# Order of the first loads and products in a fused three-layer transformer kernel

## The reference

```
proj = x @ ab_w_in[0]                    # 256 x 1024 times 1024 x 1440
c_q, c_kv, k_r, q_s, k_s, v_s = split(proj)
q  = rms_norm(c_q, q_norm) @ w_uq        # the low-rank norms
kv = rms_norm(c_kv, kv_norm) @ w_ukv
...
mem_n = rms_norm(mem_2, mem_norm_g_2[0]) # 256 x 1024, used by the third block
mk, mv = split(mem_n @ w_mem_kv_2[0])
```

## Time and profile before

| | |
|---|---|
| median of 3 runs | 922.51 us (921.9 to 922.72) |
| the profiled execution's own time | 924.75 us |
| its span in the trace | 922.6 us |
| granted TensorE clock, mean | 0.997 |
| TensorE busy | 99% of the span |
| VectorE, ScalarE, GpSimd busy | 66%, 55%, 4% |

### The profile page before, as it was taken

One profiled execution on the slowest core, in us unless ns is written; L12 is line 12 of the kernel. 1 busy time (PEld: TensorE's weight loads), 2 busy tenths in 40 slices (PEclk: granted clock), 3 DMA queues, 4 the chain that ended last, 5 costly groups with the idle time before them and its releaser, 6 DMA issues.

```text
span 922.6 us, 12818 instructions
## 1 busy us (share of the span) xinstructions
PE 911.3 (99%) x4766; PEld 765.2 (83%) x4766; DVE 608.7 (66%) x1003; ACT 508.4 (55%) x819; POOL 36.4 (4%) x53
## 2 busy tenths in 40 slices
PE   8999999999999999999999999999999999999997
PEld 6888878888888898877888888887888888888876
DVE  3788687666662766778766666376656577574665
ACT  4876664555552456666455555355457574655444
POOL 1100024100000001000000000001000000000000
PEclk9999999999999999999999999999999999999999
DMA  8664466755574668444755557454564565545651
GB/s 293 238 220 121 122 226 194 262 183 185 192 246 131 146 172 256 137 155 166 256 176 187 195 189 245 125 198 142 185 204 137 160 195 167 163 152 189 197 174 64
DMA packets 72556, 169.39 MB, mean 184 GB/s; under 512 B 11304, under 2 KB 33216, under 8 KB 71856
## 3 DMA queue, kind: packets, MB, share of 16 engines
q1 hardware_dynamic: 69536, 155.83, 52.2%
q0 software_dynamic: 2816, 12.48, 4.1%
q10 hardware_dynamic: 144, 0.26, 0.1%
HBM read 167.49 MB, written 1.06 MB: 183 GB/s over the span
## 4 chain that ended last, share of the span: by engine, by line
PE 95%; DVE 2%; ACT 1%; DMA 1%; issue 0%; SPq 0%; ACTq 0%; DVEq 0%
PE psum L740 21%; PE psum L927 14%; PE psum L693 8%; PE psum L688 8%; PE psum L690 8%; PE psum L931 7%; PE psum L960 7%; PE psum L965 3%; PE psum L851 3%; PE psum L861 3%; PE psum L855 3%; PE psum L1062 2%; PE psum L1093 1%; PE psum L660 1%; PE psum L1076 1%; PE psum L1018 1%
## 5 line engine op out<-in xcount | busy, mean ns | idle before, releaser
L1636 DVE TENSOR_TENSOR base_lo<-stage,base_hi 128x1024 fp32r<-128x1024 f32 (+3 forms) x222 | 262.1, 1204 | 95.1 <-ACT base_hi L1245 94.2
L1245 ACT CAST base_hi<-stage 128x1024 fp32r<-128x1024 f32 (+3 forms) x222 | 223.8, 1035 | 52.4 <-PE psum L693 25.3
L1636 DVE TENSOR_TENSOR extra_lo<-stage,extra_hi 128x1024 fp32r<-128x1024 f32 (+1 forms) x68 | 80.0, 1202 | 47.5 <-ACT extra_hi L1245 47.4
L688 PE MATMUL psum<-base_hi,xt 128*128 128x512 f32 (+2 forms) x272 | 107.8, 396 | 1.6 <-ACT base_hi L1459 0.7
L690 PE MATMUL psum<-base_lo,xt 128*128 128x512 f32 (+2 forms) x272 | 105.2, 387 | 1.2 <-DVE base_lo L1636 0.7
L693 PE MATMUL psum<-base_hi,xt 128*128 128x512 f32 (+2 forms) x272 | 105.3, 387 | 0.0
L1245 ACT CAST extra_hi<-stage 128x1024 fp32r<-128x1024 f32 (+1 forms) x68 | 68.1, 1030 | 49.3 <-PE psum L740 33.5
L740 PE MATMUL psum<-base_hi,ht 128*128 128x512 f32 x288 | 87.3, 393 | 0.0
L927 PE MATMUL psum<-xt,extra_hi 128*128 128x512 f32 x320 | 87.3, 394 | 0.0
L960 PE MATMUL psum<-xt,base_hi 128*128 128x512 f32 x240 | 76.5, 403 | 0.0
L927 PE MATMUL psum<-xt,base_hi 128*128 128x512 f32 x256 | 69.7, 394 | 0.0
(11 more groups left out here) (243 smaller groups left out, 1548.2 us busy)
## 6 DMA issues: line engine op xcount, KB each, us to landing
stage<-in_w_up SPq DMA_DIRECT2D x80, 512.0 KB, 4.5
stage<-in_w_down SPq DMA_DIRECT2D x44, 512.0 KB, 4.5
stage<-in_w_in_a SPq DMA_DIRECT2D x22, 512.0 KB, 4.9
stage<-in_w_cd_in SPq DMA_DIRECT2D x16, 512.0 KB, 4.7
stage<-in_w_in_b SPq DMA_DIRECT2D x12, 512.0 KB, 3.6
stage<-in_w_ab_in SPq DMA_DIRECT2D x11, 480.0 KB, 6.8
ln_par<-in_ln POOLq DMA_DIRECT2D x4, 1024.0 KB, 6.6
stage<-in_w_ab_out SPq DMA_DIRECT2D x8, 512.0 KB, 3.7
```

The costliest lines, as they stand in the source:

```text
L688: pe.matmul(acc, ah, wh, start=(k == 0), stop=False)
L1245: act.copy(w_hi(c, 0, w), stage_of(c, w)).then_inc(hi_done, 1)
L1636: dve.tensor_tensor(w_lo(c, 0, w), stage_of(c, w), w_hi(c, 0, w).bitcast(F32), ALU.subtract).then_inc(lo_done, 1)
```

## The change

SyncE loads x's tile 1 behind chunk 1, ahead of chunks 2 and 3. Column step 0 has three passes: tile 0 by chunks 0 and 1, tile 1 by chunks 0 and 1, both tiles by chunks 2 and 3; the turning of a tile stands ahead of its first pass. ScalarE and VectorE turn and split in the order that goes with it. Memory's norm row, memory and the gains are loaded by SyncE behind chunk 7, and no longer by GpSimd, which still loads the heads' parameters there.

```diff
--- before.py
+++ after.py
@@ -505,6 +505,9 @@
             u = PRODUCTS[name].u0 + steps - 1
             return acc_free[u % 2], TT * (u // 2 + 1)
 
+        def row(src, n):
+            return bass.AP(tensor=src.tensor, offset=src.offset, ap=[[0, P], [1, n]])
+
         block = ctx.enter_context(nc.Block())
 
 
@@ -513,6 +516,13 @@
 
             def load_x(t):
                 sp.dma_start(x[:, t, :], d["x"][t * P:(t + 1) * P, :]).then_inc(loaded[f"x{t}"], 16)
+
+            def load_memory():
+                for name, dst, src in (
+                        ("mem_g", row_g[:, :], row(d["mem_norm_g"], D)),
+                        ("mem", mem_x, d["mem"].rearrange("(t p) n -> p t n", t=TT)),
+                        ("gains", gains, row(d["gains"], Q_RANK + KV_RANK))):
+                    sp.dma_start(dst, src).then_inc(loaded[name], 16)
 
             load_x(0)
             sp.dma_start(ident[:, :], d["ident"]).then_inc(loaded["ident"], 16)
@@ -545,8 +555,10 @@
                         for m, landed in enumerate((first_staged, staged[STAGE[0]])):
                             cut = slice(m * FIRST, (m + 1) * FIRST)
                             sp.dma_start(stage_of(0, WIDTH[0])[:, cut], d["w_ab_in"][0][:, cut]).then_inc(landed, 16)
-                    if g.c0 + n == NS - 1:
+                    if g.c0 + n == 1:
                         load_x(1)
+                    if g.c0 + n == 2 * NS - 1:
+                        load_memory()
             for t in range(TT):
                 for j in range(2):
                     cut = slice(j * 512, (j + 1) * 512)
@@ -562,14 +574,8 @@
             def load(name, dst, src):
                 pool.dma_start(dst, src).then_inc(loaded[name], 16)
 
-            def row(src, n):
-                return bass.AP(tensor=src.tensor, offset=src.offset, ap=[[0, P], [1, n]])
-
             pool.memset(no_mask[:, :], 0.0).then_inc(constants_set, 1)
             pool.wait_ge(hi_done, NS)
-            load("mem_g", row_g[:, :], row(d["mem_norm_g"], D))
-            load("mem", mem_x, d["mem"].rearrange("(t p) n -> p t n", t=TT))
-            load("gains", gains, row(d["gains"], Q_RANK + KV_RANK))
             load("heads", head_par[:, :, :].rearrange("p a h -> p (a h)"), row(d["head_par"], 16))
             pool.wait_ge(hi_done, 2 * NS)
             load("swa", table, d["swa"])
@@ -665,14 +671,15 @@
 
                 u, cps = g.u0 + j, g.kc // g.kp
                 pair = u % 2
-                passes = [(t,) for t in range(TT)] if second else [tuple(range(TT))]
-                for tiles in passes:
-                    if second:
+                passes = [(tuple(range(TT)), range(cps))]
+                if second:
+                    passes = [((0,), range(2)), ((1,), range(2)), (tuple(range(TT)), range(2, cps))]
+                for tiles, chunks in passes:
+                    if second and len(tiles) == 1:
                         second(tiles[0])
                     if u >= 2:
-
-                        pe.wait_ge(acc_free[pair], 2 * (u // 2) - (tiles == (0,)))
-                    for m in range(cps):
+                        pe.wait_ge(acc_free[pair], 2 * (u // 2))
+                    for m in chunks:
                         n = j * cps + m
                         c = g.c0 + n
                         for kk in range(g.kp):
@@ -1454,12 +1461,16 @@
             turn_part(first, "x0")
             act.wait_ge(first_staged, 16)
             act.copy(w_hi(0, 0, FIRST), stage_of(0, FIRST)).then_inc(first_hi, 1)
-            turn_part(last, "x0")
             act.wait_ge(staged[STAGE[0]], 16)
             act.copy(w_hi(0, FIRST, FIRST), stage_of(0, WIDTH[0])[:, FIRST:]).then_inc(hi_done, 1)
             done["chunks"] = 1
+            turn_part(last, "x0")
+            split_to(2)
+            first, last = turn_parts("x0", [1])
+            turn_part(first, "x0")
+            split_to(3)
+            turn_part(last, "x0")
             split_to(NS)
-            turn("x0", xt_hi, 0, [1])
 
             def memory_norm():
                 act.wait_ge(constants_set, 3)
@@ -1972,8 +1983,12 @@
             split_first(1).then_inc(lo_done, 1)
             done["chunks"] = 1
             turn_part(last, xt_hi, xt_lo, 0, "x0")
+            split_to(2)
+            first, last = turn_parts("x0", [1])
+            turn_part(first, xt_hi, xt_lo, 0, "x0")
+            split_to(3)
+            turn_part(last, xt_hi, xt_lo, 0, "x0")
             split_to(NS)
-            turn("x0", xt_hi, xt_lo, 0, [1])
 
             def memory_norm():
                 dve.wait_ge(loaded["mem_g"], 16)
```

## The result

The changed kernel took **925.86 us** (median of 6 runs, 924.27 to 927.07), the kernel before, beside it, 922.06 (6 runs, 921.73 to 922.72). The ratio is 1.0033, 95% interval 1.0021 to 1.0045: slower, by 3.8 us, where 921.9 was forecast with 920.8 to 924.0 as the range. Its traced execution took 927.07 us with a span of 925.1, where the span before was 922.6. Four of all the executions told of here, one of them of the kernel before, took 1130 to 1876 us; they are left out of the ratios and move a median by 0.1 us at most.

The account below looks back on a forecast made before the run. TensorE, busy 99% of the span, was taken as the bound; 0.55 us saved there, all else costing nothing, turned the profiled 924.75 us into 924.2, and the median 922.51 into 921.9, range 920.8 to 924.0.

Parts of the forecast that it names:

- Memory on the weights' queue: Memory's loads on SyncE behind chunk 7: chunk 8 lands at about 28.7 us instead of 27.4, hidden, costing nothing.
- rival B: Memory ahead of chunk 8 delays ScalarE if under 0.37 MB/us: +1.05 us at 300 GB/s, +2.85 at 243; chance 0.15.
- The passes: Column step 0 on TensorE: the new pass order shrinks the hole at tile 1's start from 0.70 to 0.15, saving 0.55 us.
- rival C: Hole before tile 1's first product only moves if TensorE turns tile 1 at full clock; median stays 922.5; chance 0.10.
- Chunks 2 and 3 split later: ScalarE and VectorE split these chunks around tile 1's turn, still 0.7 and 1.5 us early for TensorE; cost nothing.
- Rival A: Transposes in the 1.2 GHz stretch keep TensorE's clock low for longer: +1.0 us, 923.5; chance 0.16.
- Rival D: TensorE's clock doesn't fall at 12 us: -1.7 and -0.55 us, giving 920.3; chance 0.07.

Follow-up runs that it names:

- e3: The changed kernel with memory's three loads on SyncE behind chunk 5 instead of chunk 7; 922.33 us, kernel before 922.64, ratio 0.9995.
- e4: The changed kernel with GpSimd asking for the 1.5 MB table and the rope table at chunk 9's highs instead of chunk 7's; 924.19 us, ratio 1.0019 to before.
- e9: The changed kernel once more, without an edit, on another chip; 925.86 us, kernel before 922.48, ratio 1.0037.
- e2: The kernel before with only memory's three loads moved to SyncE's queue behind chunk 7, old passes; 922.4 us, kernel before 922.64, ratio 0.9998.
- e5: The kernel before with only x's tile 1 loaded earlier, behind chunk 1; 924.41 us, kernel before 922.6, ratio 1.0016.
- e10: e7 with memory's three loads moved back behind chunk 7, as in the change; 922.62 us, ratio 1.0002 to the kernel before.
- e7: e3 with tile 1 turned between two products of tile 0, in TensorE's wait for chunk 1's lows; 921.32 us, kernel before 922.6, ratio 0.9983.
- e8: e3 with unread products of ones in TensorE's waits between 8 and 12 us; 922.42 us, ratio 0.9998 to the kernel before.

## Why the prediction was wrong

- **The step that failed is "Memory on the weights' queue".** It put chunk 8 at 28.7 us and the price at nothing; chunk 8 came at 30.84 and the price was some 3.5 us of the 3.8 (e3 against the change: 922.33 and 925.86). Chunk 7 was asked for 1.1 us earlier than forecast (18.22, not 19.3) and yet landed 0.7 later (23.7, not 23.0), as it took 5.5 us and not the first transfer's 3.7. Between the landings of chunks 7 and 8 I counted 2.39 MB at 0.42 MB/us, 5.7 us; it took 7.1, 0.34 MB/us for these four loads. The engines were hardly slower than I took them, they moved 404 GB/s, but 0.39 MB of it were GpSimd's table, which the sum left out: 0.9 us, as e4 has it too (6.2 us without). The remaining 0.5 are about 0.09 MB of other packets and the 404 in place of 420. The 0.34 is inside rival B's condition (under 0.37), and B is what happened, by its place and by its sign. In a sentence apart: the Trainium skill (DMA: Bandwidth & Descriptors, section Bandwidth) gives 341 GB/s for a 1 MB load from GpSimd, by which chunk 8 would land at 30.0. The trace has 335 GB/s over the four loads, and that it comes so near is luck, since the engines moved 404 GB/s in this time.
- **The same step left out a term, GpSimd's table.** Chunk 9 was taken to be ready behind memory's squares. It landed 4.5 us behind chunk 8, because the table, which starts when ScalarE has copied chunk 7, now met it on the engines. e4 gives that its price: 1.7 us between the medians, 1.5 at the eviction, counted from memory's issue. With both, the eviction was 3.3 us late; B at 300 GB/s, which gave chunk 8 at 31.0, had only 1.6 for it.
- **"The passes" was right for one kind of execution, and that kind is rare.** With the clock down the saving is 0.6 (e4) and 0.2 (e9), 0.55 forecast. With the clock up it is nothing: from chunk 1's lows to step 1 it takes 10.63 us after and 21.17 - 10.46 = 10.71 in e2. That is rival C. I knew that the traced execution, 924.75, stood 2.24 us above the median; the step was to ask whether the stretch at 1.2 GHz that I saw in it is in the median execution. By their mean clock 19 of 108 executions of before have it.
- **"Chunks 2 and 3 split later"** cost nothing at TensorE, as forecast: it had no idle time from 16 to 33 us. But these splits also free the stages of chunks 6 and 7. With the order of before, the queue had a gap of 6.5 us between chunk 7 and chunk 8 (e2) into which memory would have fit. The prediction had both times, 19.3 and 20.4, and did not read them against the times of before.
- **Rival A did not come up**: in e9 and e4 transposes lie in the low stretch, and it is 3.4 us as before. In e4 three products stood behind the transposes before the clock rose; in e9 it rose at about 14.4, while the transposes (from 13.08 on) still ran, with products ahead of them. In a sentence apart: what the Trainium skill (TensorE: Matmul & The Clock Gate, Part 4) holds of transposes was to speak for A; no run here lengthened the stretch, nor does any show transposes alone keeping or raising the clock. **Rival D** is how the traced execution after ran, but most of before's run so as well, so it is no effect of the change. Its sum also took the 0.55 us together with a clock that stays up, where by rival C's own condition there is nothing to save.

What stays open: why the engines move only 225 to 294 GB/s from 18 to 24 us, the stretch in which chunk 7 lands late, and whether e5's loss at full clock, 1.8 us by the medians, is more than the 1.2 us worked out for it.

## What to carry to other kernels

Before a transfer is put into a queue, look for the gap that is to take it: the time between the neighbours' issues in the new order, not in the old one. Here 1.9 MB cost nothing in a gap of 6.5 us and 3.5 us in one of 1.5, with the same neighbours, and the gap closed through the other half of the same change. The gap alone doesn't give the price: in e10 it is 1.5 us too and the cost, against e7, is 1.3, since the queue is asked earlier. So carry the landing of the next transfer on to the engine that wants it, and count what other queues move in that time. And when the traced execution stands above the median, find what is in it that the median has not, before counting a saving there.

## What the hardware did that I had not expected

- From 18 to 24 us, with chunks 6 and 7 and the first of memory's loads under way, the changed kernel moved 225, 235 and 294 GB/s in windows of 2 us, and 404 GB/s between the landings of chunks 7 and 8. That the queue had run empty before doesn't explain it: in e10 it hadn't, and its window from 16 to 18 us has 125. The row of 0.5 MB to all partitions is among what was asked for; no run separates it from the rest.
- A table of 1.5 MB on GpSimd's queue slowed SyncE's: the same four loads took 7.1 us with it (7.2 in e9) and 6.2 without (e4), and chunk 9 came 4.5 us behind chunk 8 with it and 1.2 without.
- A stretch of 3.4 us at 1.2 GHz that begins between 10.9 and 12.2 us is in the traced executions of before, e4, e5 and e9 and in none of the other traced ones: the changed kernel ran once without it and once with it (e9). e8 filled idle time ahead of it with products and was no faster in the median.
- GpSimd's affine select stretched four VectorE scalings of 128x128 from 1.01 to 1.61 us when it lay upon them, and to 1.58 to 1.65 in five further traces.
